# The last block's product P1 goes among the last up products, into a weight buffer of its own, and a half read goes ahead of an operand

## What is computed

```
def squared_relu_mlp(h, w1, w2):
    return jnp.square(jax.nn.relu(h @ w1)) @ w2
...
    for i in range(DEPTH):
        ...
        h = rmsnorm(x, norm_ffn_g[i])
        x = x + squared_relu_mlp(h, ffn_w1[i], ffn_w2[i])
    return rmsnorm(x, final_norm_g)
```

## Time and profile before

| | us |
|---|---|
| median of 3 runs | 1162.18 |
| lowest, highest | 1161.82, 1162.69 |
| the profiled execution | 1160.81 |
| its span, first to last instruction | 1159.0 |
| TensorE busy in the span | 1134.8 (98%) |
| VectorE, ScalarE, GpSimd busy | 810.3, 653.6, 212.0 |

### The profile page before, as it was taken

One profiled execution on the slowest core, in us unless ns is written; L12 is line 12 of the kernel. 1 busy time (PEld: TensorE's weight loads), 2 busy tenths in 40 slices (PEclk: granted clock), 3 DMA queues, 4 the chain that ended last, 5 costly groups with the idle time before them and its releaser, 6 DMA issues.

```text
span 1159.0 us, 16201 instructions
## 1 busy us (share of the span) xinstructions
PE 1134.8 (98%) x6556; PEld 1000.2 (86%) x6556; DVE 810.3 (70%) x923; ACT 653.6 (56%) x811; POOL 212.0 (18%) x196
## 2 busy tenths in 40 slices
PE   9999999999999999899999999999999999999996
PEld 7988889999999999688888888888999999999974
DVE  7887646686786776677487645664668678677677
ACT  6764445765655565655444443544576565556565
POOL 0040012112111120212164012001311211112030
PEclk9999999999999999999999999999999999999999
DMA  9532143899789785856232622313489978978585
GB/s 353 206 97 91 50 146 73 198 245 197 190 175 213 171 153 115 214 118 198 89 98 81 217 96 73 109 37 146 77 221 231 206 182 179 211 167 153 125 157 146
DMA packets 50378, 179.75 MB, mean 155 GB/s; under 512 B 5632, under 2 KB 6016, under 8 KB 49664
## 3 DMA queue, kind: packets, MB, share of 16 engines
q0 software_dynamic: 20064, 70.26, 33.6%
q1 hardware_dynamic: 28656, 104.35, 27.1%
q10 hardware_dynamic: 1584, 4.10, 1.1%
HBM read 173.45 MB, written 2.10 MB: 151 GB/s over the span
## 4 chain that ended last, share of the span: by engine, by line
PE 83%; DVE 7%; ACT 4%; DMA 3%; issue 2%; POOL 1%; SPq 0%; ACTq 0%; DVEq 0%; POOLq 0%
PE psum L2004 12%; PE psum L2006 11%; PE psum L2005 11%; PE psum L2264 8%; PE psum L2266 8%; PE psum L2265 8%; PE psum L2284 7%; PE psum L2285 7%; PE psum L2286 7%; DMA w_sum<-in_down 3%; ACT w_hi L748 1%; DMA w_raw<-in_weights 1%; PE psum L2201 1%; DVE w_lo L1253 1%; PE psum L2323 1%
## 5 line engine op out<-in xcount | busy, mean ns | idle before, releaser
L1253 DVE TENSOR_TENSOR w_lo<-w_sum,w_hi 128x1024 fp32r<-128x1024 f32 x112 | 136.0, 1223 | 82.2 <-ACT w_hi L748 82.1
L2284 PE MATMUL psum<-w_lo,slot_hi 128*128 128x512 f32 x448 | 176.0, 393 | 9.8 <-ACT staged L979 5.0
L2285 PE MATMUL psum<-w_hi,slot_hi 128*128 128x512 f32 x448 | 175.5, 392 | 0.0
L2286 PE MATMUL psum<-w_hi,slot_lo 128*128 128x512 f32 x448 | 174.9, 390 | 0.0
L748 ACT ACTIVATE w_hi<-w_sum 128x1024 fp32r<-128x1024 f32 x112 | 117.6, 1054 | 93.7 <-PE psum L2286 52.8
L2264 PE MATMUL psum<-xs_s_lo,w_hi 128*128 128x256 f32 x512 | 145.4, 284 | 2.7 <-ACT kept_p L925 2.7
L2266 PE MATMUL psum<-xs_s_hi,w_lo 128*128 128x256 f32 x512 | 144.9, 283 | 0.0
L2265 PE MATMUL psum<-xs_s_hi,w_hi 128*128 128x256 f32 x512 | 144.9, 283 | 0.0
L1253 DVE TENSOR_TENSOR w_lo<-w_raw,w_hi 128x1024 fp32r<-128x1024 f32 x80 | 97.6, 1222 | 41.9 <-ACT w_hi L748 41.7
L748 ACT ACTIVATE w_hi<-w_raw 128x1024 fp32r<-128x1024 f32 x80 | 83.8, 1055 | 69.0 <-PE psum L2266 56.8
L1942 POOL DMA_DIRECT2D w_sum<-in_down x64 | 58.6, 942 | 343.9 <-DVE w_lo L1253 343.8
(11 more groups left out here) (236 smaller groups left out, 2662.4 us busy)
## 6 DMA issues: line engine op xcount, KB each, us to landing
w_raw<-in_weights SPq DMA_DIRECT2D x89, 512.0 KB, 3.7
w_sum<-in_down POOLq DMA_DIRECT2D x64, 512.0 KB, 7.7
w_sum<-in_down SPq DMA_DIRECT2D x48, 512.0 KB, 4.5
w_raw<-in_up POOLq DMA_DIRECT2D x48, 512.0 KB, 6.6
w_raw<-in_up SPq DMA_DIRECT2D x32, 512.0 KB, 3.9
up<-in_up SPq DMA_DIRECT2D x16, 512.0 KB, 4.5
up<-in_up POOLq DMA_DIRECT2D x16, 512.0 KB, 6.9
y_rows<-staged POOLq DMA_DIRECT2D x6, 512.0 KB, 8.0
```

The lines of the kernel that those rows point to most:

```text
L1253: dve.tensor_tensor(w_lo[:, c % RING, :], buffer(kind, SUM_BUFFER[STAGE[p][0]] + half), w_hi[:, c % RING, :].bitcast(F32), ALU.subtract).t ...
L2284: pe.matmul(to, s_hi[:, k, tok], w_lo[:, c % RING, cols], start=first, stop=False, skip_group_check=True)
L2285: pe.matmul(to, s_hi[:, k, tok], w_hi[:, c % RING, cols], start=False, stop=False, skip_group_check=True)
L2286: last = pe.matmul(to, s_lo[:, k, tok], w_hi[:, c % RING, cols], start=False, stop=(kp == 1 and j == 1), skip_group_check=True)
```

## The change

The last block's D P1 leaves its place behind D3 P2 and stands between D2 P7 and U P4, in both layers. Its quarter 11 and the sums that follow in block 3 (P5, P6, P4) lie in `up_22`, free since U P7, and are loaded once U P7's low parts are made. The additions there signal semaphores of their own. P1's result goes to the rows by VectorE's `read` and isn't staged. P1, P6, P7 and P4 of block 3 use the PSUM pair 6 and 7, P2 the pair 2 and 3; slots and the banks of the next stage are changed to fit. Of the second kind: in each layer ScalarE's first half `keep` of P5 in block 0 stands ahead of the operand of P4, not behind it and a weight chunk.

```diff
-LAST_DOWN = (("P2", 0), ("P1", 0), ("P1", 1), ("P5", 0), ("P5", 1), ("P3", 0), ("P3", 1), ("P6", 0), ("P6", 1),
+LAST_DOWN = (("P2", 0), ("P5", 0), ("P5", 1), ("P3", 0), ("P3", 1), ("P6", 0), ("P6", 1),
              ("P2", 1), ("P7", 0), ("P7", 1), ("P4", 0), ("P4", 1))
...
+LAST_UPS = tuple((kind, FB - 2 + (kind == "U"), p) for p in ("P1", "P2", "P5", "P3") for kind in "DU") + (
+    ("U", FB - 1, "P6"), ("D", FB - 2, "P6"), ("U", FB - 1, "P7"), ("D", FB - 2, "P7"), ("D", FB - 1, "P1"),
+    ("U", FB - 1, "P4"), ("D", FB - 2, "P4"))
...
-READS[FB - 1] = ("P3", "P6", "P2", "P7", "P4")
-STAGED = ((FB - 2, "P4"), (FB - 1, "P1"), (FB - 1, "P5"))
+READS[FB - 1] = ("P1", "P3", "P6", "P2", "P7", "P4")
+STAGED = ((FB - 2, "P4"), (FB - 1, "P5"))
...
-LAST_SLOTS = {"P2": 0, "P5": 1, "P1": 2, "P3": 2, "P6": 1, "P7": 2, "P4": 1}
+LAST_SLOTS = {"P1": 0, "P2": 1, "P5": 0, "P3": 2, "P6": 0, "P7": 2, "P4": 0}
...
-    return {PAIR_X: PAIR_A, PAIR_Y: PAIR_E if p == "P2" else PAIR_Y}[ROWS_PAIR[p]]
+    return {PAIR_X: PAIR_E, PAIR_Y: PAIR_A if p == "P2" else PAIR_Y}[ROWS_PAIR[p]]
...
         for m in range(4):
-            self.add(("xt", m), "bank", at=(4, 5, 2, 3)[m])
+            self.add(("xt", m), "bank", at=4 + m)
...
-            self.row_chunk("sv", i, ST, at=(0, 1, 6, 7, 5, 2, 3, 4))
+            self.row_chunk("sv", i, ST, at=(0, 1, 2, 3, 5, 6, 7, 4))
...
-                self.add(("xt", m), "bank", at=(6, 7, 0, 1)[m - 4])
+                self.add(("xt", m), "bank", at=m - 4)
...
-    def buffer(kind, i):
-
+    def buffer(kind, b, i):
+
+        if (kind, b) == ("D", FB - 1) and i < 2:
+            return up_22[:, i, :]
...
-                for b in range(FB - 1):
+                for b in range(FB - 2):
                     for p in ("P2", "P7", "P4"):
                         refill(l, "D", b, p)
-                        if b + 1 < FB - 1:
-                            refill(l, "U", b + 1, p)
+                        refill(l, "U", b + 1, p)
+                refill(l, "D", FB - 2, "P2")
+                for half in range(2):
+                    sp.wait_ge(wlo_ready, step(l, "U", FB - 1, "P7", half) + 1)
+                    quarter(l, "D", FB - 1, "11", half)
+                refill(l, "D", FB - 2, "P7")
...
                 ahead("U", 0, "P5", 0)
+                keep(0, "P5", kept_p5, PAIR_X, half=0)
                 hi(xs["P4"][0][:], xg[:, 4:8, TOK[1]])
                 ahead("U", 0, "P5", 1)
-                keep(0, "P5", kept_p5, PAIR_X, half=0)
...
                 ahead("U", c, "P7", 0)
-                operand(c, "P2", a12, h=1)
+                operand(c, "P1", a11, h=0)
                 ahead("U", c, "P7", 1)
-                squared(c, 2, a22, "P7")
                 ahead("D", b, "P7", 0)
                 ahead("D", b, "P7", 1)
+                squared(c, 2, a22, "P7")
+                ahead("D", c, "P1", 0)
+                operand(c, "P2", a12, h=1)
+                ahead("D", c, "P1", 1)
...
                 operand(c, "P5", s1, summed=1)
-                operand(c, "P1", a11, h=0)
                 b = FB - 1
                 ahead("D", b, "P2", 0)
                 stage(0)
-                ahead("D", b, "P1", 0)
-                ahead("D", b, "P1", 1)
                 operand(b, "P3", a12, summed=3)
                 ahead("D", b, "P5", 0)
...
-                stage(1)
                 ahead("D", b, "P5", 1)
-                stage(2)
+                stage(1)
...
                 read(b, "P6")
+                operand(c, "P1", a11)
+                ahead("U", c, "P7", 1)
+                ahead("D", b, "P7", 0)
+                c22(c)
+                ahead("D", b, "P7", 1)
+                ahead("D", c, "P1", 0)
+                read(b, "P7")
                 operand(c, "P2", a12)
-                ahead("U", c, "P7", 1)
-                c22(c)
-                ahead("D", b, "P7", 0)
-                ahead("D", b, "P7", 1)
+                ahead("D", c, "P1", 1)
                 ahead("U", c, "P4", 0)
-                read(b, "P7")
+                read(c, "P1")
                 ahead("U", c, "P4", 1)
...
-                        elif p != "P6":
-                            add_staged(l, ("P1", "P5", "P3").index(p))
+                        elif p in ("P5", "P3"):
+                            add_staged(l, ("P5", "P3").index(p))
...
                 down_product(b, "P7")
+                kept_done(c, "P3")
+                down_product(c, "P1", fresh=True)
                 sum_done(c, "P7")
                 up_product(c, "P4")
                 read_done(b, "P7")
                 down_product(b, "P4")
                 b = FB - 1
-                kept_done(b, "P3")
+                kept_done(b, "P4")
                 down(b, "P2", 0, fresh=True).then_inc(psum_ready, 1)
-                kept_done(b, "P4")
-                down_product(b, "P1", fresh=True)
                 read_done(b - 1, "P3")
                 down_product(b, "P5", fresh=True)
...
-                pe.wait_ge(staged_ready, 6 * l + 4)
+                read_done(b, "P1")
                 down_product(b, "P6")
```

More of the change, by code:

```diff
@@ L72, in mlp_steps @@
             steps += [("D", b, p, h) for h in range(2)] + [("U", b + 1, p, h) for h in range(2)]
-    steps += [(kind, FB - 2 + (kind == "U"), p, h) for kind, p in LAST_UPS for h in range(2)]
+    steps += [(kind, b, p, h) for kind, b, p in LAST_UPS for h in range(2)]
     return tuple(steps + [("D", FB - 1, p, h) for p, h in LAST_DOWN])
@@ L326, in mlp_order @@
             if b >= 0:
-                for p in ("P5", "P3", "P6", "P7", "P4") if b < FB - 1 else ("P5", "P1", "P3", "P6", "P7", "P4"):
+                for p in ("P5", "P3", "P6", "P7", "P4"):
                     self.add((f, b, p), "hi", "lo")
             if b < FB - 1:
-                for p in ("P1", "P2") if b < FB - 2 else ("P2",):
+                for p in ("P1", "P2"):
                     self.add((f, b + 1, p), "hi", "lo")
@@ L430, in trunk_kernel @@
     last_s2 = at(z_off, "last_s2", [P, 4, NMEM])
-    staged = [at(a_off + 16 * KB + 4 * KB * i, f"staged_{i}", [P, 2, 512]) for i in range(3)]
+    staged = [at(a_off + 16 * KB + 4 * KB * i, f"staged_{i}", [P, 2, 512]) for i in range(len(STAGED))]
     edge_lo = at(region(GROUPS * PAD * 4), "edge_lo", [P, GROUPS, PAD], F32R)
@@ L522, in trunk_kernel @@
     quarter_added = [sem(f"quarter_added{i}") for i in range(4)]
+    last_added = [sem(f"last_added{i}") for i in range(2)]
     up_loaded = [sem(f"up_loaded{i}") for i in range(6)]
@@ L537, in trunk_kernel @@
     staged_ready = sem("staged_ready")
-    rows_added = sem("rows_added")
+    rows_added = [sem(f"rows_added{i}") for i in range(len(STAGED))]
     tile_ready = sem("tile_ready")
@@ L632, in quarter @@
                 source, loaded = (up_d, up_loaded) if kind == "U" else (down_d, quarter_loaded)
-                sp.dma_start(buffer(kind, i), source[FB * l + b, 2 * QUARTERS.index(name) + half]).then_inc(loaded[i], 16)
+                sp.dma_start(buffer(kind, b, i), source[FB * l + b, 2 * QUARTERS.index(name) + half]).then_inc(loaded[i], 16)
             def refill(l, kind, b, p):
@@ L744, in hi_quarter @@
                     act.wait_ge(loaded[i], 16 * (FB * l + b + 1))
-                else:
-                    sums = 3 if part == "sum" else 1
-                    act.wait_ge(adds[i], 16 * (sums * (FB * l + b) + added))
-                act.activation(w_hi[:, c % RING, :], buffer(kind, i), ACT.Copy).then_inc(whi_ready, 1)
+                elif part != "sum":
+                    act.wait_ge(adds[i], 16 * (FB * l + b + added))
+                elif kind == "U":
+                    act.wait_ge(up_added[i], 16 * (3 * (FB * l + b) + added))
+                elif b < FB - 1:
+                    act.wait_ge(quarter_added[i], 16 * (3 * ((FB - 1) * l + b) + added))
+                else:
+                    act.wait_ge(last_added[i], 16 * (3 * l + added))
+                act.activation(w_hi[:, c % RING, :], buffer(kind, b, i), ACT.Copy).then_inc(whi_ready, 1)
             def hi_any(c):
@@ L1252, in lo_any @@
                 dve.wait_ge(whi_ready, c + 1)
-                dve.tensor_tensor(w_lo[:, c % RING, :], buffer(kind, SUM_BUFFER[STAGE[p][0]] + half),
+                dve.tensor_tensor(w_lo[:, c % RING, :], buffer(kind, b, SUM_BUFFER[STAGE[p][0]] + half),
                                   w_hi[:, c % RING, :].bitcast(F32), ALU.subtract).then_inc(wlo_ready, 1)
@@ L1938, in add_quarters @@
                 source, added = (up_d, up_added) if kind == "U" else (down_d, quarter_added)
+                if kind == "D" and b == FB - 1 and part == "sum":
+                    added = last_added
                 for half in range(2):
@@ L1941, in add_quarters @@
                     pool.wait_ge(wlo_ready, step(l, kind, b, p, half) + 1)
-                    pool.dma_start(buffer(kind, i), source[FB * l + b, 2 * QUARTERS.index(name) + half],
```

(3 more changed lines are left out.)

25 lines of the change are left out of this document (8 added, 17 removed).

## The result

The changed kernel takes 1148.2 us (median of 4 runs, 1147.84 to 1148.68), the kernel before beside it 1162.43 (median of 4, 1161.82 to 1165.84); the ratio is 0.9872, 95% interval 0.9852 to 0.9891. It is faster by 14.2 us by the medians and 14.9 by the ratio, where 12.0 were forecast: 1162.18 times the ratio is 1147.3, just under the range's lower end of 1147.6. The median of the runs, 1148.2, lies within it; the two figures differ mostly by one run of the kernel before, 1165.84 us, which pulls up the mean (the ratio of the means is 0.9872 too) and not the median.

The account below looks back on a forecast made before the run. TensorE's idle time, at the ends set by the weights' chain through GpSimd's accumulating DMAs, was the bound. Layer 0's end 6.3, layer 1's 4.0 and starts 1.7 give 12.0 us off the median 1162.2: 1150.2 us, range 1147.6 to 1153.4.

Parts of the forecast that it names:

- P1's operand: Ends of both layers: the waits ahead of P1, 0.96 us in layer 0 and 1.10 in layer 1, go.
- P3: Ends of both layers: P3 starts 0.6 us late in layer 1 and 0.2 in layer 0.
- P7: Layer 1's end: the 1.08 us wait ahead of P7 goes, unless the addition lands over 1 us later.
- The half read: First up block of each layer: P3 starts 0.85 us earlier, then bound by VectorE's a11; twice 0.85 is 1.7 us.
- P1's read by VectorE: Ends of both layers: two added VectorE instructions, 1.40 us per layer, cost nothing.
- P4 in layer 1: Layer 1's end: 0 to 1.0 us of wait ahead of P4, 0.5 taken, from the last addition's landing plus 4.3.
- layer 0's end: End of layer 0's MLP: 6.6 us of idle and slow clock less 0.1 and 0.2, so 6.3 us won.
- rival 2: Whole change: no wait is left, all 14.6 us go, 1147.6 us; chance 7%.
- Rival 1: Layer 1's end: the additions still set it, so it gives 1.0 us in place of 4.0, 1153.2 us; chance 13%.
- Rival 3: Layer starts: the half read wins nothing (1151.9 us) or 1.33 us (1149.2); 6% outside the forecast's span.
- rival 4: P5 waits in P1's place as long as P1 did; layer 0 gives up to 6 us less, 1156 us; chance 3%.
- Rival 5: Ends of both layers: additions take longer than 2.9 us each, at 4.0 the kernel is slower, 1165 us; chance 3%.

Follow-up runs that it names:

- loads_small: The kernel before with layer 0's four loads for the gate cut from 512 to 32 KB each, for timing alone; 1160.18 us, ratio 0.9977.
- filled: The kernel before with four matmuls of constants, results thrown away, run while TensorE waits ahead of layer 0's P3; 1160.44 us, ratio 0.9989.

## Why the prediction came out as it did

**Right: the bound and the mechanism.** TensorE's idle time was all there was to win, and it went where the steps said. *P1's operand*: no gap is left ahead of it; P5's, in its place, shows none either (0.1 and 0.2 taken), though 8.17 us met 8.16. *P3*: 0.31 and 0.28, for 0.2 and 0.6. *P7*: none, as said. *The half read*: 0.90 us in each layer for 0.85, stopped by a11 as said. *P1's read by VectorE*: nothing, and staging it instead costs under 1 us. The sum of these and P4 was 12.0 us against the profiled execution, and that trace pair shows 12.3.

**Too small: P4 in layer 1.** I took 0.5 us of wait, 1.0 at most; it was 1.35, and 1.18 in the second trace. The step put it on the landing alone (landing, then 4.3 us). That rule fits: the landing at 1129.20 and P4's start at 1133.46 are 4.26 us apart. But 0.5 us of wait needs the landing 3.8 us ahead of P4's place, and it came 2.75 ahead (1131.95 less 1129.20). VectorE's order from P6's end on is as long by itself: low part, read of P2, low part, gain, read. I had not added those up against P4's place. It cost 0.8 us of forecast gain.

**The term that was mis-sized: layer 0's end.** This is the step that failed. The forecast took 3.95 us of wait and 1.5 us at the lower clock from one execution, 6.3 us to be won there, and then laid the sum, unchanged, on the median of other executions, 1.4 us longer. The step said only that the execution lay under the median. Against its own execution the term was nearly right: 6.6 us were won there. In the other traces this end cost 8.5 and 5.6 us against 6.9, and the change removes it whole but for 0.31. So in the execution that lies near the median, that of 1162.63 us, the term was 8.2 us in place of 6.3. This end cost 1.6 us more there than in the first trace (8.5 for 6.9), and with that the forecast would have been 1148.6. The rest, down to the measured median of 1148.2, is within what executions of the changed kernel differ by (1147.59 to 1148.68). That the timed runs had the same long end is inferred from one traced execution near their median and from their granted clocks. The range's lower end, set by rival 2 at the 14.6 us that one trace showed, was too high for the same reason.

**An incomplete cause.** The 3.95 us were put on the chain of additions. The gate's four loads made about 2.5 of them. The change moves P1's additions clear of those loads, which the prediction did not see; the gain was there either way.

**The rivals.** Rival 1 (the additions still set layer 1's end) is out for P7, whose wait went, and for P3, which kept 0.28 us; but the third wait that it named, ahead of P4, stayed for the most part, 1.35 of 1.69 us. Rival 2 (no wait is left) gave 1147.6, close to the measured time, and that is luck: P4's wait and a11's two are left, and the time came from a longer end of layer 0. Rival 3 (the half read) and rival 4 (P5 waits in P1's place) didn't come. Rival 5 (slower transfers) is out: nothing waited long but P4. The Trainium skill's fit of 3.2 us, an estimate for 512 KB issued by GpSimd, stands in the page DMA: Bandwidth & Descriptors in the section Anatomy of one DMA, not in Bandwidth, to which the prediction put it. It stays contradicted for accumulating transfers: the shortest on a chain of waits, in `loads_small`, took 5.46 us.

## What to carry to other kernels

Where a chain of weights made by accumulating DMAs ends in several dependent products, start the chain earlier by moving its first product among work that doesn't need it; how that product's result is read matters little. Before summing against one trace, ask why its execution differs from the median: a long wait with a low clock behind it varies from execution to execution, and its removal is worth its median, not what one trace shows. Where two layers run the same code and one waits longer, look for transfers that only that one has.

## What the runs showed that was not expected

- With four plain loads of 512 KB issued 6 us ahead of it, an accumulating DMA of 512 KB landed in 7.18 to 8.47 us (five traces). With the loads cut to 32 KB it took 5.46 us, with the loads held back 5.76.
- The length of a wait alone doesn't tell whether the clock falls. It was low after 3.63, 3.95, 4.54 and 4.70 us, not after 3.05 us, and low once after 2.36 us (`filled`, layer 1). How long it stayed low varied: 10 matmuls in 3.8 us in one trace, 14 in 6.0 in another.
